# First norm and product on an input with features on partitions, and the second layer's residual kept that way

## The reference, cut to what matters

```python
def rms_norm(x, gain):
    x32 = x.astype(jnp.float32)
    y = x32 * lax.rsqrt(jnp.mean(x32 * x32, axis=-1, keepdims=True) + NORM_EPS)
    return (y * gain.astype(jnp.float32)).astype(x.dtype)

def hybrid_layer(x, ...):                       # layer 1
    h = rms_norm(x, mix_norm_gain)
    proj = jnp.einsum('bsd,de->bse', h, w_in)
    ...                                         # branches, merged
    x = x + jnp.einsum('bsd,de->bse', merged, w_out)                      # x2
    h2 = rms_norm(x, ffn_norm_gain)
    gate, up = jnp.split(jnp.einsum('bsd,df->bsf', h2, w_gate_up), 2, axis=-1)
    return x + jnp.einsum('bsf,fd->bsd', jax.nn.silu(gate) * up, w_down)  # x3
# first_block then gives rms_norm(x3, final_norm_gain)

def mixer_sublayer(x, ...):                     # layer 2
    h = rmsnorm(x, norm_g)
    proj = h @ w_in
    ...                                         # hyena and fourier mixers, head norm -> y
    return x + y @ w_out                                                  # x4
# then x4 + hierarchical_moe(rmsnorm(x4, norm2_g), ...), and rmsnorm(., final_g)
```

## Time and profile before

| | us |
|---|---|
| Runs | 1049.44, 1051.56, 1051.91; median 1051.56 |
| Span of the profiled execution | 1050.5 (1.06 under the median; only the span is known of that execution) |
| PE busy | 923.8 (88% of the span) |
| DVE busy | 510.8 (49%) |
| ACT busy | 238.6 (23%) |
| POOL busy | 4.7 (0%) |
| DMA | 289.03 MB, mean 275 GB/s |

### The profile page before, as it was taken

How to read it: one execution, slowest core, us unless ns; L and a number is a source line. 1 busy time by engine, 2 the same in 40 slices (tenths; PEclk the granted TensorE clock), 3 DMA queues, 4 the chain that set the end, 5 groups by cost and what they waited for, 6 DMA issues and landing times. The chain is left out here.

```text
span 1050.5 us, 19577 instructions
## 1 busy us (share of the span) xinstructions
PE 923.8 (88%) x8288; PEld 618.3 (59%) x8288; DVE 510.8 (49%) x1283; ACT 238.6 (23%) x498; POOL 4.7 (0%) x11
## 2 busy tenths in 40 slices
PE   9999999999999999999999987976767776677686
PEld 7986467764499999644696445543334433343343
DVE  4894546578785555568568474321222212221122
ACT  2015223462221111000311232312121121221213
POOL 0100000000000000000000000000000000000000
PEclk9999999999999999999999999988888888888889
DMA  9744420035244444753165879999999999999995
GB/s 370 295 175 162 160 83 2 1 153 206 109 169 161 161 170 179 297 195 111 49 265 235 350 304 402 424 434 430 428 427 434 435 428 429 427 432 435 429 426 223
DMA packets 22839, 289.03 MB, mean 275 GB/s; under 512 B 2688, under 2 KB 4480, under 8 KB 8192
## 3 DMA queue, kind: packets, MB, share of 16 engines
q1 hardware_dynamic: 22784, 288.23, 67.1%
HBM read 287.17 MB, written 1.05 MB: 274 GB/s over the span
## 5 line engine op out<-in xcount | busy, mean ns | idle before, releaser
L463 PE MATMUL ps<-sb_ring,sb_own 128*32 128x256 f32 x1936 | 154.1, 480 | 104.8 <-DMA sb_ring<-w_exp 101.3
L463 PEld LDWEIGHTS ps<-sb_ring,sb_own 128*32 128x32 f32 x1936 | 80.1, 137 | 176.7 <-issue 108.0
L2898 DVE TENSOR_TENSOR sb_own<-sb_own,ps 128x128 f32<-128x128 f32 x32 | 9.2, 288 | 310.6 <-ACT sb_own L1950 310.6
L1281 PE MATMUL ps<-sb_nsa,sb_ring 128*128 128x128 f32 x640 | 74.7, 275 | 0.0
L1281 PEld LDWEIGHTS ps<-sb_nsa,sb_ring 128*128 128x128 f32 x640 | 73.1, 192 | 0.0
L483 PE MATMUL ps<-sb_ring,sb_own 128*32 128x256 f32 (+1 forms) x1024 | 60.4, 375 | 4.1 <-DVE sb_own L2898 2.7
L1961 ACT ACTIVATE sb_own<-ps 128x256 f32<-128x256 f32 x32 | 12.3, 385 | 208.5 <-PE ps L463 208.5
L1281 PE MATMUL ps<-sb_hT,sb_ring 128*128 128x128 f32 x480 | 56.9, 275 | 0.0
L1281 PEld LDWEIGHTS ps<-sb_hT,sb_ring 128*128 128x128 f32 x480 | 55.3, 192 | 0.1
L814 PE MATMUL ps<-sb_ring,sb_hT 128*128 128x512 f32 (+1 forms) x128 | 50.6, 550 | 0.0
L483 PEld LDWEIGHTS ps<-sb_ring,sb_own 128*32 128x32 f32 x1024 | 30.7, 109 | 30.0 <-issue 10.7
(11 more groups left out here) (605 smaller groups left out, 1504.3 us busy)
## 6 DMA issues: line engine op xcount, KB each, us to landing
sb_ring<-w_exp SPq DMA_DIRECT2D x26, 4096.0 KB, 23.5
sb_ring<-w_exp SPq DMA_DIRECT2D x38, 2048.0 KB, 22.6
sb_ring<-w_in SPq DMA_DIRECT2D x13, 2048.0 KB, 8.4
sb_ring<-w_gu SPq DMA_DIRECT2D x11, 2048.0 KB, 8.0
sb_ring<-w_dn SPq DMA_DIRECT2D x10, 1024.0 KB, 6.9
sb_ring<-w_out SPq DMA_DIRECT2D x4, 2048.0 KB, 7.8
sb_ring<-w_branch SPq DMA_DIRECT2D x2, 2048.0 KB, 8.7
sb_ring<-cmp_w SPq DMA_DIRECT2D x1, 2048.0 KB, 8.3
```

The source lines that it names most:

```text
L463: m = pe.matmul(ps[group(j), 2, 0:256], hgT[:, k, :], w[j // 2][k][:, (j % 2) * 256:(j % 2 + 1) * 256], start=(k == 0), stop=(k == KT - 1))
L1281: m = pe.matmul(out[:, i, :], w[:, k, i * P:(i + 1) * P], h[:, k, :], start=start and i == 0 and k == 0, stop=(k == KT // 2 - 1), skip_gro ...
```

## The change

- `x` is loaded a second time, as `xT` (features on partitions), into the memory of `x`, in two halves, after `cols`; the old `x` follows when the fifth block of `w_in` is loaded. The 16 transposes at the start are gone. ACT squares `xT` (128x1024 twice), PE sums the squares over features by 8 matmuls against ones, 32 columns wide in four column groups, and one of 128x256; ACT takes the root, DVE a reciprocal of 128x256. The sums stand between parts of the first product. `left_sums` of the first block moves behind the scaling of `hT`.
- After x2 has been turned for the norm, ACT copies it to `xT` (4 times 128x512), and the first piece of gate and up waits for that.
- The down product is turned round: `w_down` (or a sum of its blocks) is the weights, the activations stream: four matmuls of 128 columns for one of 512. The seven terms are regrouped; DVE's sums have the sizes they had.
- x3 and x4 are sums in `xT`. The 16 transposes each of x3 and x4, the copies to `hT` and the row sums of squares are gone. In their place stand matmuls against ones or squared gains (8 of 32 columns each), two tiny ones (`row_totals`) that turn a row of sums, and for x3 two more of 128 columns to spread a second scale. The projection of the fourier part runs by token block and half.
- The residual of layer 2 is gained by ACT (8 times 128x256, behind the copies of x1) and scaled by POOL (`tensor_tensor` 128x1024 twice), which raises `residual_ready`; DVE's last sum and SP's load to `nsa` wait for it.
- The out product has weights `w_out_2` and streams y, 256 columns at a time. The logits and x4's sums of squares stand between its last parts.
- `take_x` turns x4 with 16 matmuls of 128 columns, all ahead of `logits_read`; the two fillers of `keep_clock(2)` behind it are gone. `xn` is scaled out of PSUM, ahead of ACT's exponential. `hT` is loaded after `conv_made`, `x` after `x_taken`.

The core of the diff:

```diff
@@ sync @@
-            sp.dma_start(x.rearrange("p b n -> p (b n)"), dram["x"].rearrange("p b n -> p (b n)")).then_inc(sig("x_loaded"), 16)
             sp.dma_start(cols, dram["cols"]).then_inc(sig("cols_loaded"), 16)
+            load_x(0)
...
+                        if q == 0:
+                            load_x(1)
...
             sp.wait_ge(sig("prod_ready"), since("prod_ready", 2))
+            sp.wait_ge(sig("residual_ready"), 2)
...
             sp.wait_ge(sig("x_taken"), since("x_taken", 1))
-            sp.wait_ge(sig("xn_ready"), NB)
@@ gpsimd @@
+            pool.wait_ge(sig("residual_gained"), since("residual_gained", 1))
+            pool.wait_ge(sig("scales_ready"), since("scales_ready", 1))
+            for half in range(2):
+                at = xT[:, 4 * half:4 * half + 4, :]
+                pool.tensor_tensor(at, at, spread(mix_root, 1, 4), ALU.mult).then_inc(sig("residual_ready"), 1)
@@ tensor: down @@
-                    m = pe.matmul(ps[:, SUM_BANK[j], :], *terms[j], start=(n == 0), stop=(n == N_FC - 1), skip_group_check=True)
+                    left, right = terms[j]
+                    for i in range(4):
+                        m = pe.matmul(ps[:, SUM_BANK[j], i * P:(i + 1) * P], left[:, i * P:(i + 1) * P], right,
+                                      start=(n == 0 and i == 0), stop=(n == N_FC - 1), skip_group_check=True)
@@ tensor: layer 2 @@
+            def column_sums(bank, weights_of, squared, tiles):
+
+                for k in tiles:
+                    m = pe.matmul(ps[quarter(k % 4), bank, 0:T], weights_of(k), squared(k), start=(k < 4), stop=(k >= 4))
+                return m
...
+            project_fourier(0, 0)
+            pe.wait_ge(sig("x3_squared"), 2)
+            pe.wait_ge(sig("x3_step"), 2)
+            column_sums(7, lambda k: total_weights[:, k, :], lambda k: squares_x3[:, k, :], range(KT)).then_inc(sig("x3_summed"), 1)
+            project_fourier(0, 1)
+            pe.wait_ge(sig("x3_sums_ready"), since("x3_sums_ready", 1))
+            row_totals(7, cols[:, C_TOTAL:C_TOTAL + 2]).then_inc(sig("x3_totals_made"), 1)
+            for half in range(2):
+                project_fourier(1, half)
...
+            last_mixed(0)
+            last_mixed(1)
+            logits_part(0)
+            last_mixed(2)
+            x4_sums(0)
+            logits_part(1)
+            last_mixed(3)
+            x4_sums(1)
+            logits_part(2)
+            x4_sums(2)
+            logits_part(3).then_inc(sig("logitsT_made"), 1)
+            x4_sums(3).then_inc(sig("x4_sums_made"), 1)
...
-            take_x(range(2))
-            keep_clock(2)
+            take_x(range(4)).then_inc(sig("x_taken"), 1)
+            pe.wait_ge(sig("logits_read"), since("logits_read", 1))
@@ scalar @@
+            for k in range(KT):
+                ins = act.activation(xT[:, k, :], xT[:, k, :], ACT.Copy, scale=cols[:, C_FIN + k:C_FIN + k + 1])
+            ins.then_inc(sig("residual_gained"), 1)
...
+            act.wait_ge(sig("x4_totals_made"), since("x4_totals_made", 1))
+            act.activation(stat[:, 0:NB], ps[:, 1, T:T + NB], ACT.Sqrt, bias=cols[:, C_EPS:C_EPS + 1], scale=1.0 / (32 * D)).then_inc(sig("row_root"), 1)
+            act.wait_ge(sig("x_taken"), since("x_taken", 1))
+            act.wait_ge(sig("x4_scale_ready"), since("x4_scale_ready", 1))
             for b in range(NB):
+                act.activation(xn[:, b, :].rearrange("p (q n) -> p q n", q=4), acc[:, :, b, :], ACT.Copy, scale=stat[:, b:b + 1])\
+                   .then_inc(sig("xn_ready"), 1)
@@ vector: x3 @@
+            def h3_out(half):
+
+                dve.wait_ge(sig("x3_step"), half + 1)
+                ks = slice(4 * half, 4 * half + 4)
+                dve.tensor_tensor(hT[:, ks, :], xT[:, ks, :], spread(cols[:, C_N1 + 4 * half:C_N1 + 4 * half + 4], 2, T), ALU.mult)\
+                   .then_inc(sig("h3_ready"), 1)
```

More of the change, by code:

```diff
@@ L527, in two_layer_program @@
         block = ctx.enter_context(nc.Block())
-        SIDES = [(half, b) for half in range(2) for b in range(NB)]
         IN2_SLOTS, OUT2_SLOTS = (3, 4, 5, 1), (0, 2)
@@ L1429, in inverse_transform, with project_mixed @@
                 m.then_inc(sig("conv_made"), 1)
-            def project_mixed(banks, tiles, src, first, last):
-                for b, half in banks:
-                    mix_weights(OUT2_SLOTS[half])
-                    w = ring[:, OUT2_SLOTS[half], :].rearrange("p (k n) -> p k n", n=BANK)
+            def project_mixed(units, tiles, src, first, last):
+                for u in units:
+                    mix_weights(OUT2_SLOTS[u // 2])
+                    w = ring[:, OUT2_SLOTS[u // 2], :].rearrange("p (k n) -> p k n", n=BANK)
@@ L1436, in project_mixed @@
                     for k in tiles:
-                        m = pe.matmul(ps[:, 4 + 2 * b + half, :], src[:, k % NHT, b * P:(b + 1) * P], w[:, k, :],
-                                      start=first and k == tiles[0], stop=last and k == tiles[-1], skip_group_check=True)
-                return m
-            project_fourier()
+                        for i in range(2):
+                            at = (2 * (u % 2) + i) * P
+                            m = pe.matmul(ps[:, 4 + u, i * T:(i + 1) * T], w[:, k, at:at + P], src[:, k % NHT, :],
+                                          start=first and i == 0 and k == tiles[0], stop=last and k == tiles[-1], skip_group_check=True)
@@ L1530, in take_x @@
             def take_x(quarters):
                 for q in quarters:
-                    m = pe.matmul(ps[:, 4 + q, :], ident, x[:, :, q * Q_COLS:(q + 1) * Q_COLS], start=True, stop=False, skip_group_check=True)
+                    for b in range(NB):
+                        for i in range(2):
+                            m = pe.matmul(ps[:, 4 + q, b * T + i * P:b * T + (i + 1) * P], xT[:, 2 * q + i, b * P:(b + 1) * P], ident,
+                                          start=(b == 0 and i == 0), stop=False, skip_group_check=True)
@@ L1933, in _ @@
[L1933 to L1940 removed]
+            for u in range(4):
+                act.wait_ge(sig("x4_summed"), since("x4_summed", u + 1))
+                act.activation(square_x4(u).rearrange("p (k t) -> p k t", t=T), xT[:, 2 * u:2 * u + 2, :], ACT.Square).then_inc(sig("x4_squared"), 1)
```

363 lines of the change are left out of this document (178 added, 185 removed).

## The result

| | before | after |
|---|---|---|
| Runs beside each other, median (us) | 1050.94 (4 runs, 1049.44 to 1051.91) | 1057.68 (4 runs, 1056.60 to 1058.80) |
| Ratio, 95% interval | | 1.0057 [1.0041, 1.0073] |
| Span of the profiled execution | 1050.5 | 1054.5 |
| Start of the first ring load behind the first gates | 619.56 | 626.48 |

The change makes the kernel slower by 0.57%, +6.7 us; +1.9 was forecast, and 1057.68 lies above the range, also the widest one (1056.8). The two spans differ by 4.0 only. The last line of the table tells why that is no contradiction: the point from which the transfers of the experts start is 6.92 us later, and the profiled execution of before happened to lose some 3 us behind that point.

A forecast was written before the change was run, and what follows sets the result against it. PE's path bounds the kernel until about 667 us, then the DMA of expert weights; -1.0 + 2.7 - 0.35 + 0.55 = +1.9 us gives 1053.5 us, range 1051.5 to 1055.5 (wider: 1049.0 to 1056.8).

The forecast's parts named there:

- What bounds the kernel: Whole kernel: PE's path up to about 667 us, then the transfers of expert weights; shifts ahead of the first gather move the end equally.
- The down product: Down product: 77 products, each 35 ns longer as four matmuls of 128 columns, +2.7 us (bounds 0 to +3.5).
- The start: Program start: first product begins when its weights land, about 7.0, and the sums cost little; -1.0 us (bounds -2.0 to 0).
- The head of layer 2: Head of layer 2: transposes and spreads gone, column sums, row_totals and four matmuls new; -0.35 us (bounds -1.5 to +1.5).
- The tail: Out product to choice: four matmul stages go, four come, with a longer sum-of-squares chain; +0.55 us (bounds -1.0 to +1.5).
- the first rival: Gap before the gather: without fillers the clock falls, PE 2.2 us late, 1055.7 us in all; chance 0.20.
- Residual and copies of x2: Layer 2 residual on ACT and POOL (2.4 us per product), ACT's copies of x2 in idle time: hidden, 0.
- The earlier loads: Loads into hT and x (1 MB each), issued earlier: bring nothing by themselves.
- the chain of the root: Tail: sums, L1592, row_totals, root and reciprocal follow one another; choice starts at 605.1 to 605.25 instead of 604.68.
- a rival: Start and experts: larger start gain, and PE's halt at 644.9 falls elsewhere, saving 1.45 us; 1048.3 in all, chance 0.16.

The follow-up runs named there:

- e3: Changed kernel with x4's column sums in two stages of four tiles instead of four stages of two; 1058.05 us, ratio 1.0067.
- e5: Changed kernel with two fillers behind the wait for logits_read, two behind the ranks, and x4's sums in two stages; 1055.91 us, ratio 1.0047.

## Why the prediction was wrong, step by step

The path up to the first ring load is 6.92 us longer in the trace after. It can be read off the starts shown above, each against its counterpart of before:

| stretch | forecast | measured |
|---|---|---|
| start, up to 304 us | -1.0 | +0.14 in this trace; up to 3.0 more in others |
| down product | +2.7 | +2.69 |
| head of layer 2 | -0.35 | -0.05 |
| from the second layer's projection to the choice | +0.55 | +2.14 |
| choice to gather | 0 | +0.07 |
| gather to first ring load | 0 (a rival: +2.2) | +1.93 (from 1.25 to 2.87 in four other traces) |
| sum | +1.9 | +6.92 |

**What bounds the kernel: right.** The end follows the first ring load: in eleven traces, with loads from 620.75 to 628.59, the end comes 428.0 to 428.7 us behind it. Comparing the two profiled spans would have misled, as they differ by 4.0: before is the exception, with 430.9 us behind the load. In its execution PE halted for 3.36 us near 645 and the DMA fell to 285 GB/s, while after has 449 and 403:

```profile
645.00:650.00 5.00, 5.00 (x113) 3.62 (x106) 3.23 (x16) 1.20 (x5) 0.00 (x0) 1.00 1.05 449
650.00:655.00 5.00, 4.99 (x83) 2.90 (x78) 0.33 (x2) 2.42 (x5) 0.00 (x0) 1.00 0.95 403
```

The sum also started from that span, one of the upper group, and added 1.06 us for the step to the median. On the lower group's span it would have been some 3 us lower, and further from what was measured.

**The down product: right, to 0.01 us**, by the two piece times, and the experiment in 128 columns shows that it is the width and not the turning. 68.79 against 66.10 is 4.4 ns for a record, the number that the rows gave. The Trainium skill's 2.5 ns for a matmul ("TensorE: Matmul & The Clock Gate", "Back-to-back issue gap") gives an estimate of 1.2 us, as the prediction had it, less than half of what is measured; the rows were right to be preferred.

**The start: wrong in sign.** The step that failed is "The product then starts when its weights land, about 7.0", and -1.0 with it. In its place the traces show weights that land at 7.48 to 9.65 us, in none by 7.0, and a stretch from the product's start to the second block of 15.5 us instead of the 15.1 of the forecast (14.33 before). The transposes that were removed had kept PE at work between the warm-up and the weights. With them gone PE stands idle from the end of the warm-up (5.9 to 6.9 us) until the weights land, and the bounds had no case for late weights or for the clock. In the best traces the 0.86 to 0.98 gained is spent on the sums (1.0 and 0.43, less 0.45 for the spreads) and 0.2 more. In the worst the clock falls as well. The forecast counted the transposes as work that was only in the way; they had a use there.

**The head of layer 2: as forecast within 0.3.** The column sums take 1.00 (504.99 to 505.99) instead of 0.86: a stage of narrow tiles between full ones costs some 0.14 beyond its records.

**The tail: the term that was mis-sized.** "And what is left of logits and sums is short" was wrong: it is 2.83 us (605.04 to 607.87). A stage of `x4_sums` was counted at 0.2 us, as if its records lay four side by side. With two tiles per stage only two column groups are used, and a stage takes 0.56 (606.17 to 606.73): 2 x 0.215 and 0.13 for the change of form; a stage of the logits takes 0.58. Eight such stages stand at the out product's end, three of them ahead of its last part, which ends 1.1 later than forecast (605.04 less the 2.78 by which the stages before it are late is 602.26, not 601.2). The two-stage sums gave back 1.2, which shows the size. The Trainium skill says that a change of tiling mode drains TensorE ("TensorEngine Tiling (Array Packing)", "Key Properties"), without a number; here it comes to 0.13 to 0.15 us for a stage. The other 0.9 of the 2.14 is the chain of the root. With old start and mended tail the pick of the logits stands 108.59 us behind the spectrum, where it stood 108.52 before; but the choice starts 1.75 behind the pick instead of 0.96, since it now waits for `row_totals` (0.47), the root (0.26) and the reciprocal, which before were done under the logits. That chain was forecast in kind, at 2.0 us or a little more from L1592 to the choice; it took 1.73, so it isn't what made the tail longer than forecast.

**The clock at the gather: the first rival came true**, at 0.20 of chance and 2.2 us of price; measured 1.93, and 1.25 to 2.87 in the four other traces without fillers, and the fillers remove all of it. It should have stood in the sum, which put it at nothing; "PE has been full for 600 us ahead of the gap" was no protection. The rows that spoke for it, a gap of 5 us with 0.4 us of work, were as good as those of the other terms; what was missing was to look at what the removed fillers had been doing, the same mistake as at the start.

**Residual and copies of x2: right in time.** Nothing waits for POOL (done at 535.5, needed at 578), and gates and ups start on time. POOL's 2.52 us lie by the 2.4 that were taken. What POOL does to DVE meanwhile was not foreseen; it was hidden by luck. **The earlier loads brought nothing**, as said: in stretches of 2 us the DMA moves under 10 GB/s from 618 to the first ring load.

**The groups of executions.** Two kinds of loss make them. In the changed kernel it is the start: two traces have +1.5 (weights late, clock kept) and +3.0 (weights late, clock lost) at the second block, and the spread is 0.9 to 2.2 with the old start and 0.7 to 1.5 with the longer warm-up. No execution from 1059 to 1061.5 was caught in a trace; that it is more of the same is argued, not shown. In the kernel before two traces of the upper group have halts of PE of 3.4 and 3.9 us in all, and end 2.2 to 2.9 us late by the first ring load; nine more matmuls at the head of PE's stream make the upper group vanish, and the narrow down product with its 462 more matmul records has none either (a halt of 1.11 us at 659.55 in its trace costs nothing that can be seen). That points to where PE's instruction stream stands rather than to the work. A rival is left: in the traces without the long halts the first experts also start at least 1.2 us later, so it may be the time and not the count of instructions, and no run separates the two. The forecast knew one halt from the earlier trace rows and priced it at 1.45 us in a rival.

What PE waits for in a halt no row names, but two things in the traces point the same way. The halts stand at the same instructions in both traces of before: behind the 7th record of the fourth gather (0.30 us of idle time in the first trace, 1.40 in the second) and behind the 30th record of the gates and ups that follow (3.36 and 2.54). And the profile has a DMA queue of kind "instruction" (q8), with 43 packets of 16 KB over the span, of which one moves between 645.5 and 646.0 in both traces, inside the long halt (from 644.9 and 645.7 on), and one between 636.5 and 637.0 in the second, ahead of the 1.40. So it may be that PE runs out of instructions whose transfer is held up in the full DMA. Such packets move in the traces without halts too, and no run tests this: the cause stays open.

## What to carry to other kernels

Before removing work that costs nothing on an idle-looking engine, ask what it kept alive: here fillers ahead of the gather held TensorE's clock, and without them the work behind the wait ran at half speed. Count narrow matmuls by how many column groups a stage really fills, and add the change of form for each stage. When two profiled spans differ by a few us, compare the same point on the path, not the ends.

## What the runs showed of the hardware

- TensorE's clock fell at about 10 us in one trace with 2.14 us of idle time ahead of the first product, and stayed full in another with 2.15 us, so the length of the gap alone doesn't decide. At the gather, with one gap in all traces without fillers (5 us with two small matmuls in it), it fell 2.1 to 5.4 us behind the last long run of matmuls and stayed low for 3.4 to 10.2 us (from stretches of 1 us of the five traces).
- In the traces of e3 and e5 the granted clock reads 1.00 from 2 us on, but the six records of 128x512 of the warm-up take 5.3 and 5.5 us (4.5 to 5.5 in all traces with this warm-up), where six at full speed would take 2.6 by the earlier trace rows. Go by the length of the records there.
- GpSimd's `TENSOR_TENSOR` of 128x1024 takes 2520 ns, and two `TENSOR_SCALAR` of 128x256 of DVE beside it about 1.9 and 2.4 us instead of 0.4.
- A stage of four records of 256 columns in two column groups of 32 takes 0.56 us, one of eight in four groups 0.57, one of sixteen in four groups 1.00.
- PE halts for 1.4 to 3.4 us in the middle of a run of equal matmuls, at the same instruction in two traces of one kernel, in stretches in which the DMA moves 344 to 413 GB/s. In the kernel with nine more matmuls at the head no execution shows the loss.
